# Scaling the softmax's exponentials on ScalarE or on VectorE in the attention stage of a two-layer decoder trunk

## What is computed

```python
s = jnp.einsum('bhqd,bhkd->bhqk', qi, k) * scale
s = jnp.where(kpos[None, :] <= qpos[:, None], s, -jnp.inf)
p = jax.nn.softmax(s, axis=-1).astype(v.dtype)
return jnp.einsum('bhqk,bhkd->bhqd', p, v)
```

## Time and profile before

| | |
|---|---|
| device time, median of 3 | 1064.75 us (1064.21 to 1068.41) |
| span of the profiled execution | 1062.6 us |
| TensorE matmul busy | 956.0 us (90%) |
| TensorE weight load busy | 903.1 us (85%) |
| VectorE busy | 719.5 us (68%) |
| ScalarE busy | 485.5 us (46%) |
| VectorE, slabs' low parts (L1162) | 315.7 us |
| ScalarE, slabs' high parts (L908) | 265.6 us |
| ScalarE idle ahead of the exponentials (L1063), released by L1407 | 54.2 us |
| chain that ended last, by engine | PE 58%, DVE 15%, DMA 12%, ACT 7%, issue 6% |

### The profile page before, as it was taken

One profiled execution on the slowest core, in us unless ns is written; L12 is line 12 of the kernel. 1 busy time (PEld: TensorE's weight loads), 2 busy tenths in 40 slices (PEclk: granted clock), 3 DMA queues, 4 the chain that ended last, 5 costly groups with the idle time before them and its releaser, 6 DMA issues.

```text
span 1062.6 us, 18513 instructions
## 1 busy us (share of the span) xinstructions
PE 956.0 (90%) x6874; PEld 903.1 (85%) x6874; DVE 719.5 (68%) x984; ACT 485.5 (46%) x656; POOL 41.7 (4%) x61
## 2 busy tenths in 40 slices
PE   1499798999997899999969979899999889999996
PEld 1299787987797899999969978798779789999995
DVE  5577678967686657667648767896768665766661
ACT  2353388635524543434335438753552453343431
POOL 2100000000100000000010000000010000000000
PEclk9999999999999899999999999999999989999998
DMA  8578854351257268787445985344125716778731
GB/s 333 214 261 318 295 176 120 119 159 41 80 198 278 58 221 274 263 291 259 159 167 194 333 297 169 120 121 158 41 80 195 281 53 225 265 269 289 257 106 40
DMA packets 116010, 206.57 MB, mean 194 GB/s; under 512 B 6088, under 2 KB 92264, under 8 KB 110824
## 3 DMA queue, kind: packets, MB, share of 16 engines
q1 hardware_dynamic: 108704, 154.75, 43.3%
q0 software_dynamic: 6912, 50.33, 13.0%
q10 hardware_dynamic: 328, 0.61, 0.2%
HBM read 204.64 MB, written 1.05 MB: 194 GB/s over the span
## 4 chain that ended last, share of the span: by engine, by line
PE 58%; DVE 15%; DMA 12%; ACT 7%; issue 6%; SPq 1%; ACTq 0%; DVEq 0%
PE bank L566 16%; PE bank L567 15%; PE bank L568 15%; DMA raw<-in_w_in_dram 8%; DVE w_lo L1162 4%; ACT w_hi L908 3%; DMA front<-in_w_ada_dram 2%; DMA raw<-in_w_gu_dram 2%; DVE acc L1403 1%; PE bank L632 1%; PE bank L634 1%; PE bank L633 1%; PE bank L584 1%; DVE acc L1201 1%; ACT acc L1063 1%
## 5 line engine op out<-in xcount | busy, mean ns | idle before, releaser
L1162 DVE TENSOR_TENSOR w_lo<-raw,w_hi 128x2048 fp32r<-128x2048 f32 (+2 forms) x162 | 315.7, 1962 | 142.6 <-ACT w_hi L908 139.9
L566 PE MATMUL bank<-h_hi,w_hi 128*128 128x256 f32 x1216 | 350.7, 288 | 13.0 <-DVE h_lo L1187 9.8
L908 ACT ACTIVATE w_hi<-raw 128x2048 fp32r<-128x2048 f32 (+2 forms) x162 | 265.6, 1648 | 211.5 <-PE bank L568 114.5
L567 PE MATMUL bank<-h_lo,w_hi 128*128 128x256 f32 x1216 | 347.0, 285 | 0.0
L568 PE MATMUL bank<-h_hi,w_lo 128*128 128x256 f32 x1216 | 346.7, 285 | 0.0
L566 PEld LDWEIGHTS bank<-h_hi,w_hi 128*128 128x128 f32 x1216 | 236.1, 194 | 19.3 <-issue 15.5
L567 PEld LDWEIGHTS bank<-h_lo,w_hi 128*128 128x128 f32 x1216 | 236.2, 194 | 0.1
L568 PEld LDWEIGHTS bank<-h_hi,w_lo 128*128 128x128 f32 x1216 | 236.0, 194 | 0.0
L566 PE MATMUL bank<-y_hi,w_hi 128*128 128x256 f32 x480 | 135.5, 282 | 0.0
L567 PE MATMUL bank<-y_lo,w_hi 128*128 128x256 f32 x480 | 135.2, 282 | 0.0
L568 PE MATMUL bank<-y_hi,w_lo 128*128 128x256 f32 x480 | 135.0, 281 | 0.0
(11 more groups left out here) (179 smaller groups left out, 1053.3 us busy)
## 6 DMA issues: line engine op xcount, KB each, us to landing
raw<-in_w_gu_dram SPq DMA_DIRECT2D x88, 512.0 KB, 5.1
front<-in_w_ada_dram POOLq DMA_DIRECT2D x16, 1536.0 KB, 7.0
raw<-in_w_in_dram SPq DMA_DIRECT2D x24, 1024.0 KB, 5.8
raw<-in_w_down_dram SPq DMA_DIRECT2D x22, 1024.0 KB, 7.0
raw<-in_w_in_dram SPq DMA_DIRECT2D x32, 591.0 KB, 5.8
front<-in_w_ada_dram POOLq DMA_DIRECT2D x16, 1024.0 KB, 6.4
front<-in_w_ada_dram SPq DMA_DIRECT2D x8, 1024.0 KB, 7.4
raw<-in_w_out_dram SPq DMA_DIRECT2D x8, 1024.0 KB, 5.1
```

What stands on the lines that cost most here:

```text
L566: nc.tensor.matmul(b_out, st_hi, mv_hi, start=start, stop=False, skip_group_check=True)
L567: nc.tensor.matmul(b_out, st_hi, mv_lo, start=False, stop=False, skip_group_check=True)
L908: nc.scalar.activation(w_hi[:, slot, 0:n], raw[:, slot, 0:n], ACT.Copy).then_inc(hi_ready.sem, 1)
L1162: nc.vector.tensor_tensor(w_lo[:, slot, 0:n], raw[:, slot, 0:n], w_hi[:, slot, 0:n], ALU.subtract)\
```

## The change

The two multiplications of `normalize` are taken off VectorE. VectorE still takes the reciprocal, and raises a new event, `rinv_done`, with no wait behind it. ScalarE gets a function `weights(n)`, which waits for `rinv_done` and does the two multiplications as copies with a column of numbers as scale; the second raises `p_ready`. It is called in step n+1, behind the exponentials of head n+1 and ahead of the copy of the transposes. `DVE_LINKS` falls from 88 to 72, since 16 waits a layer are gone. TensorE's stream is the same.

```diff
--- before.py
+++ after.py
@@ -184,7 +184,7 @@
 GATE_STEPS = [1, 3, 5, 8, 10, 12, 15, 18]
 
 GATE_AT = {GATE_STEPS[2 * i + 1]: 8 + i for i in range(4)}
-DVE_LINKS = 88
+DVE_LINKS = 72
 ACT_LINKS = 6
 
 
@@ -354,6 +354,7 @@
         maxed = event("maxed", NH)
         ttr_done = event("ttr_done", 2 * NH)
         exped = event("exped", 2 * NH)
+        rinv_done = event("rinv_done", NH)
         p_ready = event("p_ready", NH)
         p_tp = event("p_tp", NH)
         pt_out = event("pt_out", NH)
@@ -1064,9 +1065,18 @@
                                              bias=negmax[n % 2][:, t:t + 1], scale=slope,
                                              accum_out=rowsum[n % 2][:, t:t + 1]).then_inc(exped.sem, 1)
 
+                def weights(n):
+                    act.wait_ge(rinv_done.sem, rinv_done.at(l, n + 1))
+                    for t, (c0, c1) in enumerate(((0, P), (P, P + T))):
+                        ins = nc.scalar.activation(p_sb[n % 4][:, c0:c1], p_sb[n % 4][:, c0:c1], ACT.Copy,
+                                                   scale=rinv[n % 2][:, t:t + 1])
+                    ins.then_inc(p_ready.sem, 1)
+
                 for n in range(NH + 4):
                     if n < NH:
                         expo(n)
+                    if 1 <= n <= NH:
+                        weights(n - 1)
                     if 2 <= n <= NH + 1:
                         act.wait_ge(p_tp.sem, p_tp.at(l, n - 1))
                         if n >= 4:
@@ -1409,11 +1419,7 @@
 
                 def normalize(n):
                     dve.wait_ge(exped.sem, exped.at(l, 2 * n + 2))
-                    link(nc.vector.reciprocal(rinv[n % 2], rowsum[n % 2]))
-                    for t, (c0, c1) in enumerate(((0, P), (P, P + T))):
-                        ins = nc.vector.tensor_scalar(p_sb[n % 4][:, c0:c1], p_sb[n % 4][:, c0:c1],
-                                                      rinv[n % 2][:, t:t + 1], None, ALU.mult)
-                    ins.then_inc(p_ready.sem, 1)
+                    nc.vector.reciprocal(rinv[n % 2], rowsum[n % 2]).then_inc(rinv_done.sem, 1)
 
                 for n in range(NH + 5):
                     if n < NH:
```

## The result

The changed kernel took 1077.34 us (median of 4 runs, 1075.6 to 1078.26), the one before 1064.48 in the same set. The ratio is 1.0108, with a 95% interval of 1.008 to 1.0136: 11.5 us slower (the two medians by themselves are 12.9 apart). The forecast was 1071.5, 6.7 slower, within 1067 to 1076.5. The ratio on the 1064.75 of the forecast gives 1076.2, at the very top of that range, and the median itself lies 0.8 above it. So the direction was right and the size was about 5 us short: the range held it with 0.3 us to spare.

The account below looks back on a forecast made before the run. VectorE and a second chain bound steps 0 to 5, ScalarE's `y_hi` the odd and VectorE the even steps 6 to 11, ScalarE steps 12 to 15. 0.9 + 0.5 + 1.95 = 3.35 a layer, 6.7 in two: 1071.5 us, range 1067 to 1076.5.

Parts of the forecast that it names:

- Section B: Steps 6 to 11: odd steps end by ScalarE's `y_hi`, even ones by VectorE; +0.5 us a layer.
- section C: Steps 12 to 15: ScalarE is the bound, three pairs of scalings lengthen its row of work; +1.95 us a layer.
- section A: Steps 0 to 5, to the first pair's `y_lo`: VectorE and a second chain arrive nearly together; +0.9 us a layer.
- VectorE, per head: VectorE's normalization: dropping the two multiplications saves 0.53 us a head (0.49 to 0.57).
- ScalarE, per head: Two new scaled copies on ScalarE, of 128 and 256 columns, cost 0.30 + 0.40 = 0.70 us a head.
- The clock: TensorE's half-clock stretches could change at two places in each layer; taken to cancel in the forecast.
- Place (b): Steps 12 to 15: TensorE's idle time before step 15's gate half exceeds 3 us; 3.3 us at half clock cost 1.65.
- Place (a): Gate half of step 3: TensorE's work shifts and the low stretch does not come there; 1.4 us less in this layer.
- R1: Rival: low clock in section C in both layers, 10.0 us slower, 1074.8; chance 0.18.
- R2: Rival: the low stretch of section A goes in both layers, 3.9 us slower, 1068.7; chance 0.26.
- R3: Rival: VectorE, not `y_hi`, ends each odd step, so its relief passes through; -7.7 us, 1057; chance 0.06.
- R4: Rival: the reciprocal waits for late exponentials, so VectorE is relieved less; no more than in the forecast, within its 0.50.

Follow-up runs that it names:

- cost-only kernel: Kernel before plus two further scaled copies per head on ScalarE with nothing depending on them, VectorE still normalizing: 1078.94 us, ratio 1.0124.
- fillers: Changed kernel plus idle-time float32 matmuls on TensorE that nobody reads, 12 of them in step 15: 1063.95 us, ratio 0.9992 to the kernel before.
- relief-only kernel: Changed kernel with the multiplications left out altogether, weights unnormalized, the reciprocal releasing TensorE: 1054.67 us, ratio 0.9898 to the kernel before.

## Why the prediction came out as it did

*What bounds each section* was right, and it is what the experiments bear out most exactly. Section B's odd steps end by `y_hi` (scalings in the odd steps alone: +0.69 a pair; in the even steps alone: -0.59), section C is ScalarE's (+1.93 alone), and VectorE's relief counts in section A and in the even steps only.

*VectorE, per head.* Taken as 0.53, it is 0.59: the instruction behind the reciprocal starts after 0.08, not 0.12. That is the low end of the two rows it was set between.

*ScalarE, per head.* Taken as 0.70, it is 0.69 in the change (275.04 to 275.73), and in the cost-only kernel too. The exponentials were the right row to go by. The Trainium skill's formula ("ScalarE: Activation LUTs", What ACT_TABLE_LOAD costs) gives 386 and 492 ns for the two; the trace has 388 and 494. The Trainium skill's rule for multiplications, VectorE and not ScalarE (same page, Rules for kernel authors), holds here by 0.1 us a head, 0.59 against 0.69, which is not where the loss comes from.

*Section A*, +0.9: measured +0.82, with the low stretch in it as before; at full clock it is -0.70 (fillers, 1063.95 us). *Section C*, +1.95: measured +1.87, and 1.93 by itself. *Section B*, +0.5: the outer pairs, +0.09 each, follow from 0.69 - 0.59 = 0.10 in place of 0.17. By these terms, with section A's low stretch as it was and no other on the path, the layer costs some 3.0, near the 3.35 of the sum.

*The clock* is the step that failed, though the range held the time. The forecast named two places where it could change, and took "the two to cancel". Place (b), section C, was named rightly: the idle time grew to 3.00 us, and the stretch at half clock came in both layers. But its length was taken over from the earlier trace rows: 3.3 us, worth 1.65. It was 6.8 us, worth 2.72. Place (a), that the low stretch of section A would go, did not come in either layer (it began 8.9 and 8.6 us from the first score, before at 8.8 and 8.7). Its size was right, as the fillers show: 1.4 by the forecast, 1.52 measured. And the middle of section B was not in the sum at all: the kernel before has a low stretch there as well (25.8 us from the first score), and it was free (35.53 to the third `y_lo` with it, 35.52 without); with TensorE's work now later and the stretch twice as long, it reached `y_hi` by way of the transposes and cost 1.3 (1.40 less the queue's 0.10). So the term "clock" was 0 in the sum and 1.3 + 2.72 = 4.0 in layer 1 of the trace, beside 3.0 of the three sections; layer 2 is 6.7 longer in all. In two layers that is 13.7 against a forecast of 6.7: the three sections 0.7 less, the clock 7.7 more. Counted against the change at full clock the low stretches cost 5.5 and 5.3 a layer and the queue 1.5.

That the time still lay in the range is in part luck. R1, the dearest case of the clock, ended at 1074.8; the range reached 1076.5 because it let the scalings be dearer by 1.5 us, and they were not. The time got there by the clock. And it came out 2.2 us lower than the two stages say (11.5 for 13.7), which no run explains.

*Rivals.* R1 (1074.8) came nearest, and was given 0.18. R2 and R3 did not come; R3's mechanism is there, but only in section A and the even steps of section B, and the relief-only kernel bounds what it can be: 7.9 us at the stages. R4: VectorE waited 0.4 us in all ahead of the reciprocal for late exponentials, nothing.

*The signs to look for* held for the groups, the row of steps 12 to 14 (7.99 for a forecast of 8.1), the waits of 2.3 us, and the outer pairs. The stage was forecast at 64 and came to 68.

## What to carry to other kernels

An instruction moved to an engine that is idle on average is paid where it stands in that engine's queue: go through the steps one by one and ask which engine ends each last, and move the work only in those that end by the engine to be relieved. Here a whole move cost 1.1%, and the same move for 6 of 16 heads, with TensorE kept at work in its waits, gained 1.2% (nothing without that work). And where a change lengthens TensorE's waits, price a stretch at half clock behind each of them, at its full length, also at places where the present one is free.

## What the runs showed of the hardware

- TensorE's granted clock fell to 0.50 behind stretches in which it was thinly used, not idle throughout: busy 1.42 of 3.30 us (kernel before), 1.34 of 3.40 and 1.20 of 3.40 (changed). The longest single wait in the first of these was 1.7 us, and in the second 1.95; the last one ran into the wait of 3.00.
- A half-clock stretch inside a stage lasts 3.4 or 6.8 us in these traces. What decides between the two is open: the kernel with heads 5, 7 and 9 on ScalarE had 3.4 in one layer and 6.8 in the other, 26 us from the first score in both. For the change both late ones were 6.8 in both layers.
- A float32 matmul of 128 columns as filler takes about 0.23 us (4.6 us for 20), in two records. In the five kernels with 19 to 54 of them a layer the clock stayed at 1.00 through all but one of the ten profiled stages. 19 of them cost the kernel before nothing (61.11 for 61.10 in layer 1); the set of 54, which outlasted a wait, made the changed kernel's stage 64.2 long in place of 62.6 with 36.
- The program outside the two stages took 932 to 943 us of the profiled spans, though the kernels do the same work there, so a difference of some us in a single profile says little; the time between two `y_lo` of a stage repeats to 0.1 us between the layers, unless the clock differs.
